# Reordering the attention stage of a two-layer decoder trunk: latent products inside the last projection chunk, a compression chain spread over the first attention units

## What is computed

```python
def layer_mixers(xn, l):                       # xn = rms_norm(h)
    cq, ckv, kr, cb, cc, chv, gu, gv, nq, nkc, nvc, nks, nvs, nkw, nvw, ng = split(xn @ w_in[l])
    # MLA: q and kv from normalised latents, rotary part, causal attention (4 heads, 96 wide)
    q = rms_norm(cq) @ w_uq;  kv = rms_norm(ckv) @ w_ukv
    q, k = rope on the last 32 of 96 columns (k's are shared by the heads)
    y_mla = softmax(q k^T + causal) v
    y_conv = cb * conv3(cc * chv)
    # gMLP: 128x128 causal mixing matrix per group, for both blocks of 128 rows
    y_gmlp = gelu(gu) * (ws[g] @ layer_norm(gelu(gv)) + b_s)
    # NSA: compressed, selected and window branch (4 heads, 64 wide)
    kc = gelu((blocks(nkc) + pe) @ w1_k) @ w2_k      # 15 compressed rows; the same for vc
    o_cmp = softmax(q kc^T + mask) vc
    o_sel, o_win = two causal attentions with keys nks and nkw
    y_nsa = sigmoid(ng) * (o_cmp, o_sel, o_win)
    return concat(rms_norm of each) @ w_o[l]
```

## Time and profile before

| what | value |
|---|---|
| time, median of 3 runs | 1472.94 us (1471.33 to 1474.48) |
| the profiled execution's own time | 1472.44 us |
| its span | 1470.7 us |
| mean granted clock of TensorE | 0.978 |
| PE busy | 1396.2 us (95%) |
| DVE / ACT / POOL busy | 819.5 / 705.5 / 35.9 us |

### The profile page before, as it was taken

The page is one execution under the profiler, slowest core; times in us unless marked ns, Lnnn a source line. Parts: engine busy times, 40 slices in busy tenths (PEclk is TensorE's granted clock), DMA queues, the critical chain, the costliest instruction groups (busy, mean ns, idle before and its releaser), DMA issues.

```text
span 1470.7 us, 16634 instructions
## 1 busy us (share of the span) xinstructions
PE 1396.2 (95%) x6613; PEld 1012.9 (69%) x6613; DVE 819.5 (56%) x794; ACT 705.5 (48%) x773; POOL 35.9 (2%) x92
## 2 busy tenths in 40 slices
PE   8989999999899897999999999999999999999995
PEld 6865688888777746675756785757667757666574
DVE  4624454544354246655647675756656846547476
ACT  5454443444253523445635564545446645436363
POOL 2000000000000000000000000000000000000011
PEclk9989999999999897999999999999999999999998
DMA  9630755555343224999999999999999999999993
GB/s 342 224 115 1 258 199 180 192 174 176 137 148 126 104 86 158 410 409 409 402 409 410 403 393 394 409 411 409 409 396 410 410 409 403 409 410 409 402 403 128
DMA packets 148478, 444.37 MB, mean 302 GB/s; under 512 B 9454, under 2 KB 21612, under 8 KB 148396
## 3 DMA queue, kind: packets, MB, share of 16 engines
q1 hardware_dynamic: 146836, 438.24, 77.8%
q0 software_dynamic: 1440, 4.98, 0.8%
q10 hardware_dynamic: 120, 0.04, 0.0%
HBM read 439.30 MB, written 3.93 MB: 301 GB/s over the span
## 4 chain that ended last, share of the span: by engine, by line
PE 86%; DVE 5%; ACT 4%; DMA 2%; issue 1%; POOL 0%; DVEq 0%; POOLq 0%; SPq 0%; ACTq 0%
PE bank L821 83%; PE bank L824 3%; DVE ring_l L1772 1%; ACT part_h L1394 1%; DMA most<-in_moe_w_down_dram 1%; DMA ring<-in_moe_w_down_dram 1%; DVE most_l L1772 1%; DVE part_l L1772 0%; DVE more_l L1772 0%; ACT junk L1403 0%; ACT xh L1394 0%; ACT prob L1595 0%; DVE y L1772 0%; ACT probT L1394 0%; DVE gm L1777 0%
## 5 line engine op out<-in xcount | busy, mean ns | idle before, releaser
L1394 ACT ACTIVATE part_h<-ring 128x2048 fp32r<-128x2048 f32 x144 | 274.1, 1918 | 136.9 <-PE bank L821 132.4
L821 PE MATMUL bank<-part_h,xh 128*128 128x512 f32 x784 | 312.1, 398 | 6.1 <-DVE xl L2180 2.5
L821 PE MATMUL bank<-part_h,xl 128*128 128x512 f32 x784 | 306.2, 391 | 0.0
L1772 DVE TENSOR_TENSOR ring_l<-ring,part_h 128x2048 fp32r<-128x2048 f32 x102 | 231.6, 2289 | 49.5 <-ACT part_h L1394 48.7
L821 PEld LDWEIGHTS bank<-part_h,xh 128*128 128x128 f32 x784 | 147.6, 188 | 46.9 <-issue 8.2
L821 PE MATMUL bank<-part_h,hTh 128*128 128x512 f32 x392 | 156.2, 398 | 17.0 <-DVE ring_l L1772 10.2
L821 PEld LDWEIGHTS bank<-part_h,xl 128*128 128x128 f32 x784 | 147.5, 188 | 31.7
L821 PE MATMUL bank<-part_h,hTl 128*128 128x512 f32 x392 | 153.9, 393 | 0.0
L1772 DVE TENSOR_TENSOR part_l<-ring,part_h 128x2048 fp32r<-128x2048 f32 x42 | 96.1, 2292 | 83.8 <-ACT part_h L1394 83.8
L1772 DVE TENSOR_TENSOR part_l<-part_in,part_h 128x2048 fp32r<-128x2048 f32 x54 | 123.0, 2289 | 32.6 <-ACT part_h L1394 32.1
L821 PE MATMUL bank<-part_l,xh 128*128 128x512 f32 x360 | 140.2, 389 | 0.0
(11 more groups left out here) (320 smaller groups left out, 1837.9 us busy)
## 6 DMA issues: line engine op xcount, KB each, us to landing
ring<-in_moe_w_down_dram SPq DMA_DIRECT2D x60, 1024.0 KB, 13.9
ring<-in_moe_w_up_dram SPq DMA_DIRECT2D x58, 1024.0 KB, 14.7
ring<-in_moe_w_gate_dram SPq DMA_DIRECT2D x50, 1024.0 KB, 12.6
part_in<-in_moe_w_down_dram SPq DMA_DIRECT2D x36, 1024.0 KB, 14.0
most<-in_moe_w_gate_dram SPq DMA_DIRECT2D x27, 1024.0 KB, 14.8
part_in<-in_moe_w_up_dram SPq DMA_DIRECT2D x27, 1024.0 KB, 13.4
part_in<-in_moe_w_gate_dram SPq DMA_DIRECT2D x21, 1024.0 KB, 15.2
most<-in_moe_w_up_dram SPq DMA_DIRECT2D x17, 1024.0 KB, 13.2
```

The lines of the kernel that those rows point to most:

```text
L821: return nc.tensor.matmul(o, lhsT, rhs, start=start, stop=stop)
L1394: return nc.scalar.activation(dst, src, ACT.Copy, scale=scale)
L1772: return nc.vector.tensor_tensor(o, a, b, op)
```

## The change

1. `mix` is taken apart. Its first part, the q and kv products (`raise_latents`), and the gMLP mixing (`spatial`) are issued inside `project`, between the two halves of the last chunk. `s_qp` is raised for each block, and ACT copies each block out as it comes.
2. `spatial` makes one product of 128 columns for both blocks where there were two of 64: 4 products, not 8. It no longer waits for `s_nT`, and writes bank 1.
3. ACT's q and kv copies and mask copies, and DVE's rotary part and gMLP output, stand before the last chunk's copies out of PSUM.
4. After the projection PE runs `turn_mla`, `turn_blocks`, `turn_nsa`, `compress` (both products in a row), `scores(0)`, `turn_hidden_blocks`, `scores(1)`, `compressed_rows`, then the units.
5. The rest of the compressed branch goes into the units: compressed scores behind `values(0)`, the turn behind `values(1)`, the product behind `values(2)`; on DVE and ACT behind units 2 and 3.
6. The sums of squares of the conv and gMLP groups move from ahead of the compression copy on ACT to units 3 and 4.
7. Buffers: q, k and v lie in parts of `xs` and `y` rather than in the region of the projection's operands; `rt` lies over `conv_k`, `mask_r` over `cn`. Total size is kept by a filler, `behind`. The compressed branch uses bank 6 throughout.

The diff, cut to its core:

```diff
@@ project
                             elif b == NB - 1:
                                 i.then_inc(s_inu, 1)
+                        if p == 2 * NIN - 2:
+                            raise_latents(l)
+                            spatial(l)
+
+            def raise_latents(l):
+                pe.wait_ge(s_cT, l + 1)
+                pe.wait_ge(s_pev, NIN * l + NIN - 1)
+                for b in range(NB):
+                    for k in range(QR // P):
+                        mm(bank[2 * b][:, 0:HEADS * QK], cT[:, k, b * P:(b + 1) * P], w_uq[:, l, k, :],
+                           k == 0, k == QR // P - 1)
+                    mm(bank[(3, 7)[b]][:, :], cT[:, 2, b * P:(b + 1) * P], w_ukv[:, l, :],
+                       True, True).then_inc(s_qp, 1)
+
+            def spatial(l):
+                pe.wait_ge(s_gv, l + 1)
+                pe.wait_ge(s_yc, l + 1)
+                if l == 0:
+                    pe.wait_ge(s_ws, 1)
+                sv = bank[1][:, :].rearrange("p (b n) -> p b n", b=NB)
+                for g in range(4):
+                    c = GW + g * DH
+                    i = mm(sv[:, :, g * DH:(g + 1) * DH], wsT[:, l * 4 + g, :], gel[:, :, c:c + DH], True, True)
+                i.then_inc(s_sv, 1)
@@ scores
-                if n < 2:
+                if n == 0:
                     pe.wait_ge(s_qT, l + 1)
                     pe.wait_ge(s_mr, l + 1)
+                elif n == 1:
+                    pe.wait_ge(s_nT, l + 1)
@@ attend
+                turn_mla(l)
+                turn_blocks(l)
+                turn_nsa(l)
+                compress(l)
                 scores(l, 0)
-                pe.wait_ge(s_pc, l + 1)
-                for b in range(NB):
-                    i = turn(bank[3][:, 128 + b * P:128 + (b + 1) * P],
-                             pc[:, b, :, :].rearrange("p h c -> p (h c)"))
-                i.then_inc(s_pcp, 1)
+                turn_hidden_blocks(l)
                 scores(l, 1)
-                pe.wait_ge(s_pcT, l + 1)
-                for b in range(NB):
-                    i = mm(bank[6][:, b * GW:(b + 1) * GW], pcT[:, b, :], vcd[:, :], True, True)
-                i.then_inc(s_oc, 1)
+                compressed_rows(l)
                 for n in range(NU):
                     turn_probs(l, n)
                     if n + 2 < NU:
                         scores(l, n + 2)
                     if n == NU - 1:
                         turn_group(l, 0)
                     values(l, n)
+                    if n == 0:
+                        compressed_scores(l)
+                    if n == 1:
+                        turn_compressed(l)
+                    if n == 2:
+                        compressed_values(l)
@@ scalar, chunk NIN - 2 (the mask copies stand in chunk NIN - 3)
+                        for b in range(NB):
+                            act.wait_ge(s_qp, NB * l + b + 1)
+                            copy(q5[:, b, 0:HEADS, :],
+                                 bank[2 * b][:, 0:HEADS * QK].rearrange("p (h d) -> p h d", h=HEADS))
...
+                        i.then_inc(s_qa, 1)
@@ scalar, after the projection
-                act.wait_ge(s_yc, l + 1)
-                act.wait_ge(s_yg, l + 1)
-                group_squares(1)
-                group_squares(2)
@@ scalar, units
+                    if n == 2:
+                        act.wait_ge(s_scm, l + 1)
+                        nc.scalar.activation(pc[:, :, :, 0:NC].rearrange("p b h c -> p (b h) c"), sc[:, :, 0:NC],
+                                             ACT.Exp).then_inc(s_pc, 1)
+                    if n == 3:
+                        act.wait_ge(s_yc, l + 1)
+                        group_squares(1)
+                    if n == 4:
+                        act.wait_ge(s_yg, l + 1)
+                        group_squares(2)
@@ vector, chunk NIN - 2: behind s_yc now stand the wait for s_qa, the rotary part (s_rope),
@@ the wait for s_sv and the gMLP output (s_yg); they stood behind s_blk
@@ vector, units
                 for n in range(2, NU):
                     row_max(n)
+                    if n == 2:
+                        dve.wait_ge(s_scp, l + 1)
...
+                    if n == 3:
+                        dve.wait_ge(s_pc, l + 1)
...
+                        dve.wait_ge(s_pcp, l + 1)
```

More of the change, by code:

```diff
@@ L935, in turn_mla, with turn_blocks @@
                         turn(bank[2 * (hd // 2)][0:QK, cs], q5[:, b, hd, :])
-                        i = turn(bank[6 + hd // 2][0:QK, cs], kk[:, b, hd, :])
+                        i = turn(bank[3 + 4 * (hd // 2)][0:QK, cs], kk[:, b, hd, :])
                 i.then_inc(s_qTp, 1)
-            def mix(l):
-                pe.wait_ge(s_cT, l + 1)
-                pe.wait_ge(s_pev, NIN * l + NIN - 1)
-                for b in range(NB):
[L944 to L948, removed]
+            def turn_blocks(l):
                 out_a = NIN * (l + 1)
@@ L965, in mix, with turn_nsa, compress @@
                         for b in range(NB):
-                            i = mm(bank[1][odd * DH:(odd + 1) * DH, j * P + b * DH:j * P + (b + 1) * DH],
+                            i = mm(bank[6][odd * DH:(odd + 1) * DH, j * P + b * DH:j * P + (b + 1) * DH],
                                    proj[:, b, c:c + DH], ident[:, odd::2], True, True)
                 i.then_inc(s_zp, 1)
[L970 to L979, removed]
+            def turn_nsa(l):
+                pe.wait_ge(s_yg, l + 1)
+                for j, c in enumerate((NKS, NKW)):
+                    for b in range(NB):
+                        turn(bank[1][0:DH, j * SEQ + b * P:j * SEQ + (b + 1) * P], proj[:, b, c:c + DH])
+                for hd in range(HEADS):
+                    for b in range(NB):
+                        i = turn(bank[4 + hd // 2][0:DH, (hd % 2) * SEQ + b * P:(hd % 2) * SEQ + (b + 1) * P],
+                                 proj[:, b, NQ + hd * DH:NQ + (hd + 1) * DH])
+                i.then_inc(s_nTp, 1)
+            def compress(l):
                 pe.wait_ge(s_blk, l + 1)
@@ L1012, in mix, with turn_compressed, compressed_values @@
                         c = (b * HEADS + hd) * 16
-                        i = mm(bank[4][:, c:c + NC], nqT[0:DH, hd, b * P:(b + 1) * P], kcT[0:DH, 0:NC], True, True)
+                        i = mm(bank[6][:, c:c + NC], nqT[0:DH, hd, b * P:(b + 1) * P], kcT[0:DH, 0:NC], True, True)
                 i.then_inc(s_scp, 1)
-                pe.wait_ge(s_qT, l + 1)
+            def turn_compressed(l):
+                pe.wait_ge(s_pc, l + 1)
+                for b in range(NB):
+                    i = turn(bank[6][:, b * P:(b + 1) * P], pc[:, b, :, :].rearrange("p h c -> p (h c)"))
+                i.then_inc(s_pcp, 1)
+            def compressed_values(l):
+                pe.wait_ge(s_pcT, l + 1)
+                for b in range(NB):
+                    i = mm(bank[6][:, b * GW:(b + 1) * GW], pcT[:, b, :], vcd[:, :], True, True)
+                i.then_inc(s_oc, 1)
             def scores(l, n):
@@ L1198, in _ @@
                 project(l)
-                mix(l)
                 attend(l)
@@ L1947, in _ @@
-                for g in range(4):
-                    i = nc.vector.scalar_tensor_tensor(
-                        out=y[:, :, 2 * GW + g * DH:2 * GW + (g + 1) * DH],
-                        in0=bank[5][:, :].rearrange("p (b n) -> p b n", b=NB)[:, :, g * DH:(g + 1) * DH],
-                        scalar=columns("bs", 4 * l + g), in1=gel[:, :, g * DH:(g + 1) * DH],
-                        op0=ALU.add, op1=ALU.mult)
-                i.then_inc(s_yg, 1)
-                dve.wait_ge(s_yg, l + 1)
@@ L1956, in _ @@
-                dve.wait_ge(s_kcp, l + 1)
-                nc.vector.tensor_copy(kcT[0:DH, 0:NC], bank[3][0:DH, 0:NC])
-                for hd in range(HEADS):
-                    i = nc.vector.tensor_copy(vcd[32 * hd:32 * hd + 32, hd * DH:(hd + 1) * DH],
-                                              bank[3][32 * hd:32 * hd + 32, 64:64 + DH])
-                i.then_inc(s_kc, 1)
-                dve.wait_ge(s_gex, l + 1)
-                link(ts(gexp[:, :, :], gexp[:, :, :], 1.0, None, ALU.add))
```

165 lines of the change are left out of this document (85 added, 80 removed).

## The result

| | before | changed |
|---|---|---|
| median of 4 runs, us | 1473.64 (1471.33 to 1474.48) | 1462.74 (1461.38 to 1463.92) |
| profiled execution, us | 1472.44 | 1463.00 |
| its span, us | 1470.7 | 1461.2 |

The ratio is 0.9928, 95% interval 0.9915 to 0.9941: faster by 0.7%, 10.9 us, where 21 were forecast. The time lies 1.7 us above the range.

A forecast was written before the change was run, and what follows sets the result against it. PE sets the units' pace but waits between projection and units. Layer 0 gains 10.2 us (13.1 less 2.9), layer 1 12.8, together 23.0; less 2.0 for clock, 21.0: 1451.9 us, range 1447.5 to 1461.

The forecast's parts named there:

- The stream up to `turn_probs(0)`: PE's new order from the last chunk to unit 0: `turn_probs(0)` at 89.65, not 102.75, gaining 13.1 us in layer 0.
- the new wait for ACT: Ahead of `turn_probs(0)`, PE waits for unit 0's exponentials on ACT: 1.2 to 1.6 us.
- the two queues that were to end just in time: ACT's and DVE's queues: waits put ahead of urgent copies, all ending just in time, DVE's last projection copy at 77.0.
- The branch inside the units: Compressed scores, turns and products moved into the units: 2.9 us of PE time given back in layer 0.
- C: Rival: the interleaved branch couples the engines; half of DVE's time showing on PE gives 1455.6, all 1459; chance 0.13.
- D: Rival: transfers bind the expert stage, which does not shift; only layer 0's 10.2 us counts, 1462.7; chance 0.05.
- E: Rival: late q copies hold DVE's rotary part and PE before `turn_mla`; over 11.5 us a layer turns the sign; with no change 0.03.
- From this I take off clock: Thin stretch ahead of unit 0 and compressed scores: one clock fall allowed in the two layers, 2.0 us off 23.0.
- B: Rival: clock falls during the turns or thin stretch in both layers, about 10 us; gain 13, 1459.5; chance 0.17.

The follow-up runs named there:

- e1: Changed kernel with one product of 128 columns standing for each layer's eight compressed-score products, so computing from wrong scores: 1456.08 us, ratio 0.9893.
- e6: Changed kernel with the q, kv and gMLP products put back behind the last chunk, ahead of `turn_mla`: 1482.48 us, ratio 1.0052 to the kernel before.
- e10: Changed kernel with the compressed scores issued ahead of `scores(1)`, and DVE's copies for them ahead of `row_max(1)`: 1457.32 us, ratio 0.9888.
- e2: Changed kernel with five unused dense products of 512 columns in PE's wait ahead of `turn_probs(0)`: 1457.37 us, ratio 0.9881.
- e4: Changed kernel with the compressed scores behind `values(4)` and the rest of the branch behind `values(5)` and `(6)`: 1457.81 us, ratio 0.9916.
- e12: Changed kernel with compressed scores two at a time behind `values(0)` to `(3)`, branch's rest later, wait filled as in e2: 1448.90 us, ratio 0.9838.
- e13: e12 with one unused dense product of 512 columns behind each of `values(0)` to `(5)`: 1451.98 us, ratio 0.9848.
- e9: e1 with e2's five dense products in the wait ahead of unit 0: 1442.32 us, ratio 0.9784.
- e5: Changed kernel with unused dense products behind `turn_blocks`, ahead of unit 0, behind the compressed scores and behind `values(1)` to `(5)`: 1457.71 us, ratio 0.9886.
- e8: Kernel before with dense products in its waits for the compression copy (10), the GELUs (2) and the compressed keys (4): 1466.21 us, ratio 0.9948.

## Why the prediction was wrong, point by point

**The stream up to `turn_probs(0)`** was right: 21.8 us against 22.9. The joined gMLP products took 1.05 (forecast 1.0), the new wait for ACT 1.32 (1.2 to 1.6); the two queues that were to end just in time did.

**The branch inside the units** cost PE about what was forecast as long as the clock stood: 23.34 us without the narrow products (e1, layer 0) and 1.95 for them is 25.3, where 24.6 were forecast. PE has no gap there: busy 6.84 of 6.84 and 13.80 of 13.80 us. And the idle time that is left in the units is the old one, 0.94 us in each layer (31.93 of 32.87 in layer 0) against 0.99 in the earlier trace rows. C is refuted. So is D: behind the units all was shifted. Its time, 1462.7, is the measured one to 0.1 us, but by luck: D has layer 1 give nothing, and it gave 7.4. E did not occur.

**The step that failed** is "From this I take off clock", with "one fall in the two layers" at "2.0". The units took 32.87 and 31.18 us (87.76 to 120.63, 475.30 to 506.48) against 24.6: 8.3 and 6.6, together 14.9, or 0.7 of it by the branch's own size in each layer and the other 13.5 by the clock. The account closes: 23.0 forecast ahead of the clock, plus 2.2 for the earlier start of the units, less 14.9 is 10.3; the runs show 10.9.

**Why that step failed.** It named the place rightly (the thin stretch and "the compressed scores, 15 columns wide") and priced it by the wrong pair of rows. The price of 1.6 us came from the shortest fall of the old attention stages (first line). The longer ones were left to B: 9.55 us at 0.53 in the earlier trace rows, and in layer 1 the second line, across the old compressed scores:

```profile
470.80:474.20 3.40, 3.40 (x29) 2.12 (x31) 1.13 (x4) 0.00 (x0) 0.00 (x0) 0.50 0.00 0
...
481.10:494.70 13.60, 11.47 (x47) 10.66 (x48) 3.74 (x14) 3.77 (x14) 0.00 (x0) 0.50 0.48 186
```

The 23.0 us took for granted that both of these would go with the waits. Falls of their length came back, in the units. In the kernel before, the narrow products met a clock that had already fallen (they took 3.59), the level was back when the units began, and the units ran at 1.00. Moved into the units, the same products bring the level down themselves. Once lost there it stays lost for long, whatever brought it down: 13.7 us (changed), about 20 (e1, layer 1), over 31 (e6). That the small products behind them (turned probabilities, 64-column values) are the reason is not shown: in e10 wide ones followed, and the fall still lasted 10.2 us.

**B** was right in kind, and so was its size, 10 us of the lower clock's cost against the 13.5 measured; its time, 1459.5, is 3.2 under the result. Its place was wrong: neither the turns nor the wait alone, but in both layers the stretch behind the narrow products. The turns in a row are cleared by the changed kernel's window over `turn_mla`, `turn_blocks` and `turn_nsa`:

```profile
74.47:78.51 4.04, 4.02 (x47) 3.50 (x44) 2.44 (x9) 2.05 (x4) 0.00 (x0) 1.00 0.02 4
```

4.0 us of turns, nearly nothing else, and the clock at 1.00. `turn_mla` (1.91) and `turn_nsa` (1.50) are transposes proper; `turn_blocks`, 0.75 between them, is made of plain products with a selection matrix. The Trainium skill, "TensorE: Matmul & The Clock Gate", Part 4: PE-mode transpose, has transposes not count as a busy PE; the trace doesn't bear this out for a stretch of this length. The drain that the Trainium skill, "ScalarE: Activation LUTs", What ACT_TABLE_LOAD costs, adds to a table switch didn't show either: the load began at 84.80, took 1.28, and the next activation began at 86.09.

**What is shown and what is not.** Shown: with the narrow products in one row a fall follows behind them in the units (changed, e2, e4, both layers), and with them spread none does up to the units' end (e12, e13, both with the wait filled); a fall can begin in the wait ahead of unit 0 without them (e1, layer 1); with both out the kernel is at least 16.5 us faster for the clock alone (e9). Open: why e5 fell in spite of its fill; what brings the level down at the units' end; why some executions of one kernel have a fall that others have not, as the spread of the runs of e1, e4 and e12 over 8 us and more suggests (one execution of each was profiled); and what brings the level back. e2 is e12 without the spreading: the fill alone gave 5.4 us, both 13.8. The spreading alone, without the fill, was not tried.

## What to carry to other kernels

When an order is packed more tightly, ask of each moved group not only which wait it ends but what it does to the clock of all that PE does behind it: a row of products with few columns cost here some three times its own time (1.95 us, and in layer 1, where its fall stood alone, 31.18 less 25.3, or 5.9, of clock). Try such products two at a time among larger ones, and a few dense products, useless if need be, in the waits that remain; the two together gave 13.8 us here. Read the granted clock by stretches in the trace before, and price a fall by the longest one that it shows, not by the shortest.

## What the runs showed of the hardware

- The same units, in one execution, took 23.34 us at 1.00 and 32.46 at 0.70: once with the upper level kept through the wait ahead of them, once with it lost there (e1).
- A PE that is busy all the time does not by this regain the upper level. The window of e6 (PE busy 31.39 of 31.39 us, clock 0.50):

```profile
100.80:132.19 31.39, 31.39 (x111) 24.95 (x110) 6.92 (x18) 13.09 (x51) 1.60 (x2) 0.50 0.00 0
```

- Work added made a kernel faster: sixteen unused products in each layer of the kernel before took 8.3 us off (e8), and e6, whose move of the early products shows as a wait of 2.9 us in layer 0, cost 20 in two layers.
- A small spread between four or five runs does not mean that the clock holds. It was 2.5 us with a long fall in both layers of the profiled execution (changed), 9.6 and 8.4 where one of the two layers had a long fall (e1, e12), and 2.3 and 2.7 where the units ran at 1.00 in both (e9, e13).
